# Two-layer hybrid backbone on one core: mixer reordered, with gate products inside the attention steps

## What is computed

```
mod = silu(cond) @ w_mod + b_mod           # 6 rows of 1024: sh1, sc1, g1, sh2, sc2, g2
h   = rmsnorm(x) * g * (1 + sc1) + sh1
q/k/v of two attentions (A, C), u/v of a gMLP (B), gl = split(h @ w_in)   # 1792 + 3*1024 columns
A, C: rmsnorm per head, rotary, attention (A: sinks, window; C: all blocks), 6 heads on 2 kv heads
B:    gelu(u) * (w_s @ rmsnorm(gelu(v)) + b_s)
merged = sum over the branches of sigmoid(gl_branch) * (o_branch @ w_o_branch)
x = x + g1 * (merged @ w_out);  h2 = rmsnorm(x)*(1+sc2)+sh2
x = x + g2 * expert_choice_moe(h2)         # 16 experts, 64 + 16 slots each
```

## Time and profile before

| what | value |
|---|---|
| median of 3 runs | 2825.93 us (2824.15 to 2835.42) |
| the profiled execution, its own time | 2830.99 us |
| its span | 2829.2 us |
| PE busy | 2528.3 us (89%) |
| PE weight loads | 1915.1 us (68%) |
| DVE busy | 1669.0 us (59%) |
| ACT busy | 1195.6 us (42%) |
| POOL busy | 378.3 us (13%) |
| mean granted PE clock | 0.929 |
| data moved by DMA | 568.76 MB, 201 GB/s |

### The profile page before, as it was taken

One profiled execution on the slowest core, in us unless ns is written; L12 is line 12 of the kernel. 1 busy time (PEld: TensorE's weight loads), 2 busy tenths in 40 slices (PEclk: granted clock), 3 DMA queues, 4 the chain that ended last, 5 costly groups with the idle time before them and its releaser, 6 DMA issues.

```text
span 2829.2 us, 37290 instructions
## 1 busy us (share of the span) xinstructions
PE 2528.3 (89%) x14671; PEld 1915.1 (68%) x14671; DVE 1669.0 (59%) x2087; ACT 1195.6 (42%) x1414; POOL 378.3 (13%) x265
## 2 busy tenths in 40 slices
PE   5998899999949999999959989899999499999996
PEld 1964778989936666666529448799898266666664
DVE  2346542223567888889731664522345788888885
ACT  2222332112236666667531223411122366666664
POOL 1034000000021122211110430000000201221111
PEclk9998879999969999999979976999998699999998
DMA  8144000221539999999852530002224499999996
GB/s 299 46 169 156 1 1 16 75 82 38 224 111 333 359 372 373 368 370 377 309 204 75 175 120 1 1 16 75 83 100 165 165 336 358 373 370 374 374 375 224
DMA packets 267985, 568.76 MB, mean 201 GB/s; under 512 B 7056, under 2 KB 9280, under 8 KB 267760
## 3 DMA queue, kind: packets, MB, share of 16 engines
q1 hardware_dynamic: 251856, 512.25, 50.3%
q0 software_dynamic: 14416, 49.12, 5.9%
q10 hardware_dynamic: 1584, 5.57, 0.6%
HBM read 545.36 MB, written 26.80 MB: 202 GB/s over the span
## 4 chain that ended last, share of the span: by engine, by line
PE 47%; DMA 23%; DVE 16%; issue 7%; ACT 6%; DVEq 0%; ACTq 0%; SPq 0%; POOL 0%; POOLq 0%
PE ps L628 23%; DMA ring<-in_w_down 11%; DMA ring<-in_w_up 9%; PE ps L857 6%; DVE w_lo L1440 6%; PE ps L775 5%; ACT w_hi L1090 4%; PE ps L698 3%; PE ps L617 2%; PE ps L726 2%; PE ps L715 2%; PE ps L605 1%; DVE mx L1287 1%; PE ps L706 1%; DVE EP L1260 1%
## 5 line engine op out<-in xcount | busy, mean ns | idle before, releaser
L1440 DVE TENSOR_TENSOR w_lo<-ring,w_hi 128x2048 fp32r<-128x2048 f32 x378 | 859.0, 2285 | 165.1 <-ACT w_hi L1090 162.5
L1090 ACT ACTIVATE w_hi<-ring 128x2048 fp32r<-128x2048 f32 x384 | 722.0, 1916 | 350.0 <-DMA ring<-in_w_down 169.6
L857 PE MATMUL ps<-w_hi,xT 128*80 128x512 f32 x2048 | 647.9, 395 | 5.8 <-issue 3.5
L628 PE MATMUL ps<-WH,HTH 128*128 128x256 f32 x1840 | 541.9, 295 | 3.3 <-DVE WL L1183 3.3
L628 PE MATMUL ps<-WL,HTH 128*128 128x256 f32 x1840 | 520.6, 283 | 0.0
L628 PE MATMUL ps<-WH,HTL 128*128 128x256 f32 x1840 | 518.4, 282 | 0.0
L857 PEld LDWEIGHTS ps<-w_hi,xT 128*80 128x80 f32 x2048 | 305.4, 149 | 178.7 <-issue 9.2
L857 PE MATMUL ps<-w_lo,xT 128*80 128x512 f32 x1024 | 405.1, 396 | 0.0
L857 PE MATMUL ps<-w_hi,hT 128*80 128x512 f32 x1024 | 329.6, 397 | 29.9 <-DVE hT L1446 12.6
L628 PEld LDWEIGHTS ps<-WH,HTH 128*128 128x128 f32 x1840 | 349.7, 190 | 6.8 <-DVE WL L1183 3.7
L628 PEld LDWEIGHTS ps<-WH,HTL 128*128 128x128 f32 x1840 | 353.2, 192 | 0.0
(11 more groups left out here) (173 smaller groups left out, 2618.7 us busy)
## 6 DMA issues: line engine op xcount, KB each, us to landing
ring<-in_w_gate SPq DMA_DIRECT2D x64, 2048.0 KB, 9.4
ring<-in_w_up SPq DMA_DIRECT2D x64, 2048.0 KB, 9.5
ring<-in_w_down SPq DMA_DIRECT2D x64, 2048.0 KB, 11.5
ring<-in_w_mod SPq DMA_DIRECT2D x24, 2048.0 KB, 8.1
ring<-in_w_in SPq DMA_DIRECT2D x18, 2048.0 KB, 8.3
ring<-in_w_out SPq DMA_DIRECT2D x4, 2048.0 KB, 13.8
ring<-in_w_o SPq DMA_DIRECT2D x4, 1536.0 KB, 6.9
Y<-x_save POOLq DMA_DIRECT2D x10, 512.0 KB, 3.9
```

The lines of the kernel that those rows point to most:

```text
L628: last = nc.tensor.matmul(ps[:, g % 2, 0:256], a[:, t, k], w[:, u % 2, k], start=k == 0 and i == 0, stop=k == KB - 1 and i == 2)
L857: last = nc.tensor.matmul(ps[0:CE, bank], lhs[:, a, kb], w[:, u, k], start=kb == 0 and i == 0, stop=kb == KB - 1 and i == 2)
L1090: nc.scalar.activation(w_hi[:, u % UB], ring[:, raw[0], 4 * (u % 2):4 * (u % 2) + 4], ACT.Copy).then_inc(hi_ready, 1)
L1440: TT(w_lo[:, u % UB], ring[:, raw[0], 4 * (u % 2):4 * (u % 2) + 4], w_hi[:, u % UB].bitcast(f32), ALU.subtract).then_inc(lo_ready, 1)
```

## The change

- **Modulation.** The stationary operand is padded to 32 columns and each of the 8 matmuls of a chunk goes to one of four column tiles of PE (`tile_position=(0, 32 * q)`), so a chunk leaves four partial sums on four groups of 32 PSUM partitions. A product with `fold` adds them: in the start stage per 128 columns, later one matmul per chunk (`fold_rows`).
- **QKV.** 35 groups, in pairs that share a bank (three banks). Between them on PE: the other eight modulation chunks (`MOD_AT`), their folds (`FOLD_AT`), and the transposes of branch A's q and k (`KA_AT`). Squares, sums and roots are made in whole-array instructions while the groups run; branch C and the gMLP norm follow after the last group.
- **Attention.** 30 steps, two heads (one of each kv head) per step. Branch A comes first, then C. One bank region holds the transposes of one head at a time, one bank (6) the gate group, one (7) every side product, one (5) the outputs.
- **Fill.** 42 gate groups, 40 projections, the gMLP products and the remaining transposes are spread over the steps (`FILL`), and the last loop over `FILL` puts all of a step's items into its first place, between scores and transposes. 18 gate groups and 20 projections remain for the tail. The gate order is B, A, C.
- **Memory.** `WL` is gone; the low part is written to `ringL`, a second ring. A slot is free again when its groups are done, not when the split is done. The POOL queue loads and stores the modulation bias chunk by chunk. Masks are rounded (`maskr`), so a mask product is a single pass.

```diff
-MOD2_AT = {2 * i + 1: MOD2_FIRST + i for i in range(MOD2 - MOD2_FIRST - 1)}
+SPLIT_AT = {-(-5 * u // 2): u + 1 for u in range(U_GATE - 1)}
+SPLIT_AT[15] = U_GATE
+MOD_AT = {3 + 4 * i: i for i in range(MOD2)}
+FOLD_AT = {5 + 4 * i: i for i in range(MOD2)}
+KA_AT = {25 + 2 * t: t for t in range(NT)}
...
+put(0, 0, "gate", 0)
+put(0, 0, "gate", 1)
+put(0, 0, "gate", 2)
+for n, (j, gap) in enumerate([(j, gap) for j in (1, 2, 3) for gap in (0, 2)] + [(j, 0) for j in range(4, 15)]):
+    put(j, gap, "gate", 3 + n)
+for t in range(NT):
+    put(2 + t, 0, "kc", t)
+    put(4 + t, 1, "mlp", t)
+    put(5 + t, 1, "mix", t)
...
+for n in range(2 * NT - 1):
+    put(3 * n + 4, 0, "out", n)
...
+for step in FILL:
+    step[0] = step[0] + step[1] + step[2]
+    step[1], step[2] = [], []
```

PE, modulation:

```diff
+                    for k in range(KB):
+                        q = k % 4
+                        last = nc.tensor.matmul(ps[32 * q:32 * q + 32, bank], condT[:, k], ring[:, SLOT["mod", c], k],
+                                                start=k < 4, stop=k >= 4, tile_position=(0, 32 * q))
+                def fold_rows(i):
+
+                    pe.wait_ge(part_ready, l * MOD2 + i + 1)
+                    pe.wait_ge(mrow_ready, l * MOD2 + i)
+                    nc.tensor.matmul(ps[0:2, 5], fold[:, 0:2], modpart2, start=True, stop=True).then_inc(mrow_done, 1)
```

PE, QKV stage:

```diff
+                for g in range(QG):
...
+                    group(ps[:, QBANK[b], 256 * h:256 * h + 256], u, t).then_inc(g_done, 1)
+                    if g in MOD_AT:
+                        mod_group(MOD1 + MOD_AT[g], 4)
+                    if g in FOLD_AT:
+                        fold_rows(FOLD_AT[g])
+                    if g in KA_AT:
+                        turn_qk(0, KA_AT[g])
```

PE, attention steps:

```diff
+                def turn(v):
+
+                    n = len(pair(v // 2)[3])
+                    pe.wait_ge(e_ready, l * UNITS + v + 1)
+                    if l or v:
+                        pe.wait_ge(pt_evac, l * UNITS + v)
...
+                for j in range(NP + 1):
+                    if j < NP:
+                        scores(j)
+                    for kind, i in FILL[j][0]:
+                        extra(kind, i)
+                    if j:
+                        turn(2 * j - 2)
+                    for kind, i in FILL[j][1]:
+                        extra(kind, i)
+                    if j:
+                        turn(2 * j - 1)
+                    for kind, i in FILL[j][2]:
+                        extra(kind, i)
+                    if j:
+                        weigh(j - 1)
```

ACT, QKV stage (p counts pairs of groups):

```diff
+                    if p % 2 == 0:
+                        act.wait_ge(g_done, l * QG + min(2 * p + 2, QG))
+                        qkv_out(nc.scalar.copy, p).then_inc(g_free[p % 3], 1)
+                        if p:
+                            mod_part(p // 2 - 1)
```

ACT, attention steps:

```diff
+                for j in range(NP + 1):
+                    for kind, i in FILL[j][0]:
+                        extra(kind, i)
+                    if j < NP:
+                        exps(j, 0)
...
+                    if j:
+                        turned(j - 1)
+                    if j < NP:
+                        exps(j, 1)
```

More of the change, by code:

```diff
@@ L106, with pair @@
 HQ = 6 * NT
-UNITS = NT * 12
+NP = 2 * 3 * NT
+UNITS = 2 * NP
+GROUPS_G = GU * NT
 EPS = 1e-6
 SCALE = HD ** -0.5
[L112 to L131, removed]
+def pair(j):
+    n, g = divmod(j, 3)
+    br, t = divmod(n, NT)
     if t == NS:
@@ L381, in raw_of, with evacuated @@
+        def evacuated(engine, l, p):
+            for b in range(3):
+                n = len(range(b, p + 1, 3))
+                if n:
+                    engine.wait_ge(g_free[b], l * (QP // 3) + n + 1)
         def raw_of(j, b, first, s):
@@ new lines, in weigh @@
+                def weigh(j):
+                    t, br, g, blocks = pair(j)
+                    pe.wait_ge(pt_evac, l * UNITS + 2 * j + 2)
+                    if l or j:
+                        pe.wait_ge(o_evac, l * NP + j)
+                    if j == 0:
+                        pe.wait_ge(mrow_ready, (l + 1) * MOD2)
+                    for kv in range(2):
+                        for i, b in enumerate(blocks):
+                            c = (AV, CV)[br] + 64 * kv
+                            v = cacheV[:, br, 64 * kv:64 * kv + 64] if b == NT else y[:, b, c:c + 64]
+                            last = nc.tensor.matmul(ps[:, 5, 64 * kv:64 * kv + 64], probT[:, kv, 128 * i:128 * i + 128], v,
+                                                    start=i == 0, stop=i == len(blocks) - 1)
+                    last.then_inc(pv_done, 1)
@@ new lines, in gate, with project @@
+                def gate(o):
+                    v, t = divmod(o, NT)
+                    if l or o:
+                        pe.wait_ge(gs_ready, l * GROUPS_G + o)
+                    group(ps[:, 6, 0:256], U_GATE + v, t).then_inc(gt_done, 1)
+                def project(o):
+                    s, r = divmod(o, 4 * NT)
+                    q, t = divmod(r, NT)
+                    ks = BRANCH[STAGES[s]]
+                    if r == 0:
+                        arrived(pe, l, ("o", s))
+                    side("proj", o)
+                    w = slot_as(("o", s), len(ks), D)
+                    for i, k in enumerate(ks):
+                        last = nc.tensor.matmul(ps[:, 7, 0:256], qoT[:, k, 128 * t:128 * t + 128],
+                                                w[:, i, 256 * q:256 * q + 256], start=i == 0, stop=k == ks[-1])
+                    last.then_inc(side_done, 1)
@@ new lines, in _, with exps @@
+                split(U_GATE + 1)
+                evacuated(act, l, QP - 1)
+                act.wait_ge(sq_used, l * 3 + 2)
+                act.wait_ge(side_done, l * NSIDE + SIDE["ka", NT - 1] + 1)
+                nc.scalar.activation(sqa, y[:, :, CQ:CQ + 512], ACT.Square).then_inc(sq_ready, 1)
+                root(NT + 1, rs100[:, :, 8:20], st100[:, :, 8:20])
+                def exps(j, kv):
+                    t, br, g, blocks = pair(j)
+                    n, b, v = 128 * len(blocks), j % 2, 2 * j + kv
+                    act.wait_ge(nm_ready, l * NP + j + 1)
+                    if l or v >= 2:
+                        act.wait_ge(pt_done, l * UNITS + v - 1)
+                    nc.scalar.activation(prob[:, kv, 0:n], s_pair[:, kv, 0:n], ACT.Exp, bias=nm[:, b, kv:kv + 1],
+                                         scale=SCALE, accum_out=sm[:, b, kv:kv + 1]).then_inc(e_ready, 1)
+                    if br == 0 and kv:
+                        nc.scalar.activation(es[:, b], eb[:, b], ACT.Exp).then_inc(es_ready, 1)
@@ new lines, in extra @@
+                def extra(kind, i):
+                    if kind == "gate":
+                        v, t = divmod(i, NT)
+                        if t == 0 and v:
+                            split(U_GATE + v + 1)
+                    elif kind == "proj":
+                        project(i)
+                    elif kind == "mlp":
+                        mlp(i)
+                for j in range(NP + 1):
+                    if j < NP:
+                        peak(j)
+                    for kind, i in FILL[j][0]:
+                        extra(kind, i)
+                    if j:
+                        turned(j - 1)
+                    if 1 <= j <= NT:
+                        rotate(1, j - 1)
+                    for kind, i in FILL[j][1]:
+                        extra(kind, i)
+                    if j:
+                        weights(j - 1)
+                    for kind, i in FILL[j][2]:
+                        extra(kind, i)
+                    if j:
+                        weighed(j - 1)
```

1085 lines of the change are left out of this document (565 added, 520 removed).

## The result

The changed kernel takes 2939.8 us (median of 4 runs, 2937.6 to 2949.0), the kernel before 2829.6 us in the same session (2824.2 to 2835.4): ratio 1.0395, 95% interval 1.0362 to 1.0429. It is slower by 110 us. 2857 was predicted, 31 more than the 2826 from which the prediction counts, and the measured time lies above its range (2750 to 2930).

A forecast was written before the change was run, and what follows sets the result against it. PE was taken as the bound in most stages, attention at a lowered clock. Per layer 612 us of work and waits plus 34 for clock falls made 646 against 628, 36 more in two layers: 2857 us, range 2750 to 2930.

The forecast's parts named there:

- the two waits: In each attention step PE idles before the second transposes and before the weighing; 2.2 us together with five blocks.
- I take 12 falls: 34: Attention steps: PE's clock drops 12 times per layer, each costing about 2.8 us, 34 us in all.
- the sum without the clock: PE work and waits per layer from QKV's start to the last gate group: 612 us, against 628 before.
- a fall in each of 30 steps: Rival: the clock drops in every attention step, 84 us per layer instead of 34; 2957 us, chance 0.05.
- The clock holds: Rival: no clock falls in attention, each layer 612 us; 2789 us, or 2735 if copies hide better; chance 0.32.
- 101 + 20 + 8 + 12 + 6: QKV per layer in us: groups, eight modulation chunks, their folds, fold waits, then A's q/k transposes with the gate-chunk delay.
- fold waits: In QKV each of eight folds waits 1.5 us for ACT's pair copy and partial-sum copy; 12 us per layer.
- the first gate chunk: End of QKV: loaded only after group 30, so ACT, waiting for it, delays a q/k copy; 3 us.
- 8 + 165 + 170 + 69 + 22 + 31: Per layer in us: attention entry, attention steps, gates, projections, remaining transposes with gMLP and merged tiles, waits inside the fill.
- The start: Start stage before QKV: gain of 3 us in layer 1, 2 in layer 2; bounds 15 faster to 8 slower together.
- the rival that they do not overlap: Modulation chunks in QKV gain nothing from column tiles, 36 us more per layer; 2929 us, chance 0.08.
- `w_o`: Gate stage: these weights arrive one step ahead of first use, so 15 us of waits per layer go.

The follow-up runs named there:

- the two runs: The changed kernel (2939.8 us), and the changed kernel with QKV's eight modulation chunks as full-width products instead of four column tiles (3022.1 us, ratio 1.0705).

## Why the prediction was wrong

The sign and the mechanism were right (the two waits, and a clock that falls in them); a term of the sum was too small.

- **The failed step is the clock**: "I take 12 falls: 34". There were 24 per layer. The price of a fall was near, 3.3 us measured (62 / 19) against 2.8. The granted clock was 0.85, where 0.90 to 0.94 was forecast. With 24 falls at 2.8 the term is 67, and the forecast of a layer becomes 679 against 681 measured. That it comes so near is partly luck: the sum without the clock was some 9 us too long, the price of a fall was 0.5 us too small, 24 times, and the two nearly cancel. I had set the number between two stretches of the earlier trace rows with a busy time of 2.59 and 2.27 of 4 us, one with a fall and one without. But I had written myself that the new stretch, 1.1 us of work in 3.3, "is leaner than both". A case outside both rows was put between them. The bound, a fall in each of 30 steps, was nearer the truth (its rival: 2957 us, chance 0.05), and it should have been the likeliest case.
- **The clock holds** (0.32) was the rival I trusted most, and the one furthest off. It rested on one stretch without a fall. The run with one wait filled shows how little that says: of two steps alike, one falls and one does not.
- **The sum without the clock nearly held.** 612 was forecast from QKV's start to the last gate. The run with both waits filled, which leaves the steps as long as their waits make them and takes most falls away, needs 139 + 480 = 619 with 5 falls left, so 603 without them.
- **Inside it**, QKV was 8 us shorter: 139 against 147 (101 + 20 + 8 + 12 + 6). Chunks took 1.92 us, not 2.5 (5 us less); fold waits 1.22, not 1.5 (2 less); the first gate chunk cost PE nothing that I can see. Attention to gates agrees: 480 - 5 x 3.3 = 464 against 465 forecast for its terms without the clock (8 + 165 + 170 + 69 + 22 + 31).
- **The two idles of a step**, forecast at 1.0 to 1.2 us each: the first is 1.06 in half of the five-block steps and 1.5 in the other half, where a projection ends the fill and DVE's copy comes late; the second is shorter, 0.79. Together they are 1.9 or 2.3 us, against 2.2.
- **The start** was forecast 3 us faster in layer 1 and 2 in layer 2. QKV starts 4 us later in layer 1 (81.7 against 77.9); in layer 2 it starts 72.0 us after the experts' last product, against 69.4. The 32 small products with their 8 transposes take 15.0 us, where 8 to 13 were given: the clock falls among them.
- **Column tiles**: the rival that they do not overlap (0.08) is out. The Trainium skill, TensorEngine Tiling (Array Packing), Theoretical Speedup, gives up to four times; the traces of the two runs show 7.05 / 1.92 = 3.7.
- **`w_o`**: among the releasers of the projections' waits no transfer is left, as forecast.

Not settled: how much of the 112 us that the rest of the change gains belongs to which part. Only the column tiles were measured by themselves (82 us); the clock's share of 65 us is an estimate, and since the two are more than 112 together, other parts must cost; the fold waits, some 20 us, are one.

## What to carry to other kernels

Put independent dense work between an operation and the copy that it waits for, not all of it in one block ahead; here the order alone was worth 230 of 2940 us, over half of it through the clock. When a change makes a stretch leaner than any in the trace, take the outer bound for the clock, not a value between the rows seen: here 24 falls, where 12 was taken and 30 was the bound. And a cheap test tells the two costs apart: fill the waits with products that nobody reads; what comes back is the clock, what stays is the wait.

## What the runs showed of the hardware

- Work that nobody needs made a kernel faster: some 340 more products of 256 columns per layer, 0.15 us each in their groups (1.19 / 8), took 125 us off.
- A busy PE does not keep the clock by being busy. In the start stage of the changed kernel it issued fp32 products of 2 columns without a gap; the clock went from 0.97 to 0.50 among them, and two such records went from 0.38 to 0.58 us. In the second layer it fell among them too (0.54 at us 1511, PE busy without a gap from 1499 to 1520). What it is in these products that does it was not separated. PE's busy time and granted clock in the first layer:

```profile
50.00:53.00 3.00, 3.00 (x20) 2.86 (x20) 1.33 (x1) 3.00 (x2) 0.00 (x0) 0.97 1.06 388
...
56.00:63.00 7.00, 7.00 (x28) 6.79 (x28) 0.00 (x0) 0.00 (x0) 0.00 (x0) 0.50 0.42 155
```

- Four column tiles of 32 columns ran a chunk 3.7 times faster in fp32, and the switch to them and back left no idle time of PE before or behind any of the eight chunks of QKV.
